# Spreading the inverse roots of the token norms by two r32 matmuls over a split diagonal, at other places among the tiles

## The chip, the cores and the metric

The kernel runs on one core of a Trainium2 chip. The metric is the device time of one execution in microseconds (us). Engines are named as in the profile: PE is TensorE (PEld its weight loads), DVE is VectorE, ACT is ScalarE, POOL is GpSimd, SP is SyncE, which issues the large DMAs.

## The reference, cut to what matters

512 tokens of width 1024 pass two transformer blocks in float32. What matters here is the shape that all of its norms have: a matrix product of the normalised activations, with the factor of each token pulled out of the product.

```python
def rms_norm(x, g):
    xf = x.astype(jnp.float32)
    y = xf * lax.rsqrt(jnp.mean(xf * xf, axis=-1, keepdims=True) + EPS)
    return (y * g.astype(jnp.float32)).astype(x.dtype)
...
        h = h + 0.5 * swiglu(rms_norm(h, ffn1_norm[i]), ffn1_w_gate[i], ffn1_w_up[i], ffn1_w_down[i])
        u = rms_norm(h, mix_norm[i])
        z = u @ w_in[i]
...
        gate = jax.nn.sigmoid(rms_norm(h, ple_norm[i]) @ w_ple_gate[i])
        h = h + gate * (p[i] @ w_ple_proj[i])
    return rms_norm(h, final_norm)
...
        x = x + mixers[layer % N_MIXERS](rms_norm_2(x, norm1[layer]))
        x = x + conv_ffn(rms_norm_2(x, norm2[layer]), *ffns[layer])
    return rms_norm_2(x, final_norm)
```

The mixer that is used in the second block is gated linear attention (GLA): it projects to q, k, v, a gate, and a 16-wide `a_low`, from which a second product makes the decay.

## The kernel before, in words

**Layout and precision.** Activations stand feature-major: 8 chunks (KD) of 128 features in the partitions, 512 tokens (S) in the free dimension. Each product of full precision is made of three r32 matmuls (`mm3`, L1644 to L1646): low weights by high input, high weights by low input, high by high. Weights come by DMA in slabs of 128x1024 into a ring of four (`w_raw`). ACT rounds a slab to its high part (`hi_part`, L681), POOL subtracts it for the low part in two pieces of 128x512 (`lo_part`, L594, both inputs in SBUF), and PE waits for `lo_ready` of the slab that a tile uses. A tile is 128 output features by 512 tokens, 24 matmuls, in one of four PSUM banks (`acc`); DVE evicts it and multiplies by the factor of each token (`rstd`).

**Order of the stages.** Feed-forward 1 up (44 tiles, the first four written out in `first_tiles`, L1759 to L1765), down, the mixing block in an order that is written by hand (`MIX`), feed-forward 2 up and down, the gates and the projection of the side input (`PLE_STEPS`: pgate 0, pgate 1, then eight short pproj tiles, then pgate 2 to 7), the GLA block in a hand-written order (`GLA`: gva, gk 0, alpha, gq 0, ...), feed-forward 3. Each engine walks through the same lists with semaphores between them.

**The norm of a token.** The squares are summed over the chunks by ACT and DVE; `sums(k)` on PE adds up the partitions token by token (L1655), in four columns of PSUM, so that the root is a short operation: ACT takes the square root, DVE makes the inverse root of 128x4 with a Newton step (`newton`, L1061 to L1065) in `tok_out`, a slice of PSUM. To bring it back into the form `rstd[any partition, token]`, DVE multiplies the identity by it (`spread_diag`, L1074: inputs `ident` in SBUF and `tok_out` in PSUM, output 128x512), and one fp32 matmul of ones by this diagonal matrix spreads it over all partitions (`spread(k)`, L1666). DVE copies it from PSUM to `rstd` (L1084). This is done for the norms k = 0 (before feed-forward 1), 1 (mixing), 3 (PLE gate) and 4 (GLA, which has two factors and so two diagonals and two matmuls). The other norms (`sums` with L1657, and the last one) are not touched by the change.

**Where the spreads stand.** PE goes on with tiles whose eviction needs the factor, and puts the spread among them:

- k = 0 in `first_tiles`, in tile 3 behind the low-input matmul of chunk 6 (`SPREAD_AT`).
- k = 1 in the mixing block, tile kk, ahead of chunk 6 (`mix_tile`, L1862 on).
- k = 3 in pgate 1 ahead of chunk 6 (`between` of `fm_tile`).
- k = 4 in tile gk 0 ahead of chunk 6, behind the transposes of `alow_k` (`turn_alow`, L2006). DVE makes its two diagonals between the evictions of token groups 1 and 2 of gva (evictions at L1509 and L1510).

Behind gk 0 comes `alpha`: four fp32 matmuls of 16 rows (L2036) that need `alow_ready`, a DVE copy of the transposed `alow` (L1512) that follows the gva evictions on DVE. DVE then copies `rstd` (L1514) and evicts gk 0 (L1537) and alpha (L1518).

**The start.** POOL sets `ones` and two columns of `eps` (L586 to L588, each one count of `consts_set`); PE waits for three counts and runs 16 warming matmuls on `ones` (L1840) ahead of the first tile.

Of the kernel before, what the change touches and what calls it, by code (L numbers as in the profile page):

```python
# [16 lines left out]
F32 = mybir.dt.float32  # L17
# [6 lines left out]
P = 128  # L24
# [24 lines left out]
SUMS_AT = (2, 5)  # L49
SPREAD_AT = (3, 6)  # L50
BANKS = 4
# [137 lines left out]
def layer_program(nc, A, out):  # L189
# [12 lines left out]
    with ExitStack() as ctx:  # L202
# [16 lines left out]
        rstd = sb("rstd", [P, S])  # L219
        ones = sb("ones", [P, P], side="right")  # L220
        cols = sb("cols", [P, NCOLS], side="right")
        consts = sb("consts", [P, NCONST], side="right")
        eps = sb("eps", [P, 2], side="right")
        rstd_tok = sb("rstd_tok", [P, NT], side="right")
        small = sb("small", [P, 176], side="right")
        gate_t, up_t, sq = tmp[:, 0:2, :], tmp[:, 2:4, :], tmp[:, 4:6, :]
        gres, ssum2 = side[:, 0, :], side[:, 1, :]
# [236 lines left out]
        def square(k, e):  # L464
            return tmp[:, e % 6, :] if k == 0 else sq[:, e % 2, :]

        def piece(p):

            return slice(2 * p * P, (2 * p + 2) * P)
# [115 lines left out]
        def _(pool):  # L585
            pool.memset(ones[:, :], 1.0).then_inc(consts_set, 1)  # L586
            pool.memset(eps[:, 0:1], NORM_EPS).then_inc(consts_set, 1)
            pool.memset(eps[:, 1:2], GN_EPS).then_inc(consts_set, 1)  # L588

            def lo_part(slot, width, count):  # L590
# [428 lines left out]
        def _(dve):  # L1019
# [52 lines left out]

            def spread_diag(i, tok):
                return dve.tensor_tensor(sq[:, i, :].rearrange("p (a b) -> p a b", a=NT), ident.unsqueeze(1).to_broadcast([P, NT, P]),  # L1074
                                         tok.unsqueeze(2).to_broadcast([P, NT, P]), ALU.mult)

            def rstd_by_token(roots, count, k):

                dve.wait_ge(root_ready, roots)
                link(inverse_root(tok_out[:, 0:NT], aux[:, 0, 0:NT], 1.0 / D, NORM_EPS, tok_ms[:, 0:NT], tok_root[:, 0:NT]))  # L1080
                spread_diag(0, tok_out[:, 0:NT]).then_inc(diag_ready, 1)
                dve.tensor_copy(rstd_tok[:, :], tok_out[:, 0:NT])
                dve.wait_ge(rstd_spread, SPREAD.index(k) + 1)
                dve.tensor_copy(rstd[:, :], aux[:, 1, :]).then_inc(rstd_ready, 1)  # L1084
                dve.wait_ge(rstd_ready, count)
# [410 lines left out]
            for step in GLA:  # L1496
# [5 lines left out]
                if kind == "gva":  # L1502
                    for tt in range(NT):
                        bank = acc[:, (t + tt) % BANKS, :]
                        if tt == 2:
                            spread_diag(0, tok_out[:, 0:NT])
                            spread_diag(1, tok_out[:, NT:2 * NT]).then_inc(diag_ready, 1)
                        dve.wait_ge(tile_done, t + tt + 1)
                        dve.tensor_scalar(alow_k[:, tt, :], bank[:, G_DV:GVA], rstd_tok[:, tt:tt + 1], None, ALU.mult)  # L1509
                        dve.tensor_scalar(gvt[:, 0, tt, :], bank[:, 0:G_DV], rstd_tok[:, tt:tt + 1], None, ALU.mult).then_inc(tile_freed, 1)  # L1510
                    dve.wait_ge(alow_turned, 1)
                    dve.tensor_copy(alow_t[0:G_RANK, :], aux[0:G_RANK, 3, :]).then_inc(alow_ready, 1)  # L1512
# [112 lines left out]
        def _(pe):  # L1625
# [36 lines left out]
            def spread(k):  # L1662

                pe.wait_ge(diag_ready, SPREAD.index(k) + 1)
                for i in range(2 if k == 4 else 1):
                    last = pe.matmul(aux[:, 1 + i, :], ones[:, :], sq[:, i, :], start=True, stop=True)  # L1666
                last.then_inc(rstd_spread, 1)
# [169 lines left out]
            HIDDEN = [KF, 2 * KF, 3 * KF + 2]  # L1837
            pe.wait_ge(consts_set, 3)
            for _ in range(WARM):
# [6 lines left out]
            def mix_tile(step, upto):  # L1846
# [28 lines left out]
                for c in range(first, upto):  # L1875
                    if step == ("kk",) and c == 6:
                        spread(1)
                    if step == ("wout", 0):
                        pe.wait_ge(split_ready, nth(lo_steps, (("mg", c), 0)) + 1)
                    last = mm3(o, (n % RING, blk(c)), x_hi[:, c, :], x_lo[:, c, :], c == 0, c == KD - 1)  # L1880
# [109 lines left out]
            for step in PLE_STEPS:  # L1990
                n, t = plan.first[step]
                if step[0] == "pgate":
                    fm_tile(t, [(n, b) for b in range(KD)], u_hi, u_lo, (lambda c: (u_ready, KD * 3 + c + 1)) if step[1] == 0 else None,
                            (lambda: spread(3)) if step[1] == 1 else None, u_used if step[1] == KD - 1 else None)
                    if step[1] == 0:
                        sums(3)
                else:
                    pe.wait_ge(hid_ready, 2 * KF + 2)
                    for i in range(4):
                        fm_tile(t + i, [(n, 2 * i), (n, 2 * i + 1)], p_hi, p_lo)  # L2000

            def turn_alow():
# [5 lines left out]
                free_when[3] = (alow_ready, 1)  # L2008
                spread(4)

            for step in GLA:
                kind = step[0]
                n, t = plan.first[step]
                if kind == "gva":
                    turns = [(k, tt) for k in range(2) for tt in range(NT - 1)] + [(k, NT - 1) for k in range(2)]
                    for k, tt in turns + [(k, tt) for k in range(2, KD) for tt in range(NT)]:
# [12 lines left out]
                        if k == KD - 1:  # L2029
                            last.then_inc(tile_done, 1)  # L2030
                elif kind == "alpha":
                    pe.wait_ge(alow_ready, 1)
                    pe.wait_ge(ple_loaded, 32)
# [186 lines left out]
```

## Time and profile before

| | |
|---|---|
| time, median of 3 runs | 1864.77 us (1863.76 to 1864.80) |
| time of the profiled execution | 1862.73 us |
| its span in the profile | 1860.9 us |
| PE busy | 1840.0 us, 99% |
| PE weight loads | 1498.0 us, 80% |
| DVE, ACT, POOL busy | 43%, 37%, 49% |
| mean granted clock of PE | 0.999 |
| chain that ended last | PE 96%, DVE 2%, ACT 1% |

The profiled execution is one run; 1.8 us of its time lie around the span. The start column of a timeline is in us from the start of the span, and the duration of a matmul is longer than the distance to the next start, because matmuls overlap: what a matmul costs PE is read from start to start. A merged row ("x6") has the time from the start of its first to the end of its last instruction. A released wait stands in brackets with the engine that ended it.

### The profile page before, as it was taken

How to read it: one execution, taken by the hardware profiler on the slowest of the kernel's cores; microseconds unless marked ns; L12 is line 12 of the kernel's file. 1: busy time of each engine (PE TensorE's matmuls, PEld its weight loads, DVE VectorE, ACT ScalarE, POOL GpSimd, SP SyncE). 2: the span in 40 equal slices, each digit the busy share in tenths (PEclk: the TensorE clock that was granted, in tenths of full speed). 3: DMA queues.
4: the chain of work that ended last, by engine and by line, in shares of the span. 5: the costliest groups of instructions: out<-in, count | busy, mean ns of one | idle time of the engine just before them, and what ended most of it. 6: DMA issues, size and time to landing. Idle time of an engine off the chain costs nothing.

```text
span 1860.9 us, 23896 instructions
## 1 busy us (share of the span) xinstructions
PE 1840.0 (99%) x8624; PEld 1498.0 (80%) x8624; DVE 793.1 (43%) x1297; ACT 679.4 (37%) x930; POOL 909.5 (49%) x710
## 2 busy tenths in 40 slices
PE   9999999999999999999999999999999999999998
PEld 8888888886878658888888888888877888888887
DVE  6222236215666653244222212266756374545312
ACT  5322223222232652244434422246344344444222
POOL 5544445386667424454444445353423455454542
PEclk9999999999999999999999999999999999999999
DMA  5333233243322212232232233232222222323331
GB/s 186 102 101 101 87 100 103 72 131 103 106 85 86 85 46 90 92 102 91 98 98 97 87 97 101 87 107 77 80 68 69 91 96 96 101 90 99 94 95 53
DMA packets 55093, 174.58 MB, mean 94 GB/s; under 512 B 6369, under 2 KB 10721, under 8 KB 55025
## 3 DMA queue, kind: packets, MB, share of 16 engines
q1 hardware_dynamic: 54848, 173.37, 29.4%
q8 instruction: 44, 0.72, 0.2%
q10 hardware_dynamic: 176, 0.30, 0.1%
q14 instruction: 25, 0.20, 0.0%
HBM read 166.56 MB, written 2.10 MB: 91 GB/s over the span
## 4 chain that ended last, share of the span: by engine, by line
PE 96%; DVE 2%; ACT 1%; issue 0%; DMA 0%; DVEq 0%; POOL 0%; ACTq 0%; POOLq 0%
PE acc L1644 28%; PE acc L1645 28%; PE acc L1646 28%; PE acc L1749 1%; PE acc L1751 1%; PE acc L1750 1%; PE aux L1927 1%; PE aux L1957 1%; PE acc L2079 0%; PE acc L2074 0%; PE acc L1978 0%; PE aux L1916 0%; PE aux L2065 0%; PE acc L1765 0%; PE acc L1759 0%
## 5 line engine op out<-in xcount | busy, mean ns | idle before, releaser
L594 POOL TENSOR_TENSOR w_lo<-w_raw,w_hi 128x512 fp32r<-128x512 f32 x626 | 812.6, 1321 | 911.4 <-ACT w_hi L681 911.4
L1644 PE MATMUL acc<-u_hi,w_lo 128*128 128x512 f32 x1544 | 611.7, 396 | 0.0
L1645 PE MATMUL acc<-u_lo,w_hi 128*128 128x512 f32 x1544 | 601.8, 390 | 0.0
L1646 PE MATMUL acc<-u_hi,w_hi 128*128 128x512 f32 x1544 | 601.8, 390 | 0.0
L681 ACT ACTIVATE w_hi<-w_raw 128x1024 fp32r<-128x1024 f32 (+2 forms) x313 | 321.8, 1033 | 549.6 <-PE acc L1646 472.1
L1644 PEld LDWEIGHTS acc<-u_hi,w_lo 128*128 128x128 f32 x1544 | 290.2, 188 | 71.9 <-issue 10.0
L1645 PEld LDWEIGHTS acc<-u_lo,w_hi 128*128 128x128 f32 x1544 | 290.3, 188 | 61.3 <-issue 2.6
L1646 PEld LDWEIGHTS acc<-u_hi,w_hi 128*128 128x128 f32 x1544 | 290.2, 188 | 61.2
L1644 PE MATMUL acc<-hid_hi,w_lo 128*128 128x512 f32 (+1 forms) x550 | 209.6, 381 | 0.0
L1645 PE MATMUL acc<-hid_lo,w_hi 128*128 128x512 f32 (+1 forms) x550 | 209.3, 380 | 0.0
L1646 PE MATMUL acc<-hid_hi,w_hi 128*128 128x512 f32 (+1 forms) x550 | 209.3, 380 | 0.0
L1644 PEld LDWEIGHTS acc<-hid_hi,w_lo 128*128 128x128 f32 x550 | 103.4, 188 | 19.8
L1645 PEld LDWEIGHTS acc<-hid_lo,w_hi 128*128 128x128 f32 x550 | 103.4, 188 | 19.8
L1646 PEld LDWEIGHTS acc<-hid_hi,w_hi 128*128 128x128 f32 x550 | 103.4, 188 | 19.7
L1102 DVE TENSOR_TENSOR tmp<-acc,rstd 128x512 f32<-128x512 f32 x43 | 29.7, 691 | 190.2 <-PE acc L1646 190.2
L1223 DVE SCALAR_TENSOR_TENSOR h<-acc,h 128x512 f32<-128x512 f32 x23 | 15.9, 691 | 220.5 <-PE acc L1646 220.5
L726 ACT ACTIVATE hid_hi<-tmp 128x512 f32 (+1 forms) x44 | 27.8, 633 | 211.8 <-DVE tmp L1093 211.8
L756 ACT ACTIVATE tmp<-tmp,cols 128x512 f32<-128x512 f32 x44 | 35.9, 816 | 116.2 <-DVE tmp L1130 116.2
L1130 DVE TENSOR_TENSOR tmp<-acc,rstd 128x512 f32<-128x512 f32 x44 | 30.3, 691 | 94.8 <-PE acc L1646 94.8
L1100 DVE TENSOR_TENSOR tmp<-acc,rstd 128x512 f32<-128x512 f32 x43 | 29.7, 691 | 90.5 <-PE acc L1646 90.3
L1044 DVE SCALAR_TENSOR_TENSOR u_lo<-h,cols,u_hi 128x512 fp32r<-128x512 f32 x40 | 42.6, 1076 | 36.5 <-ACT u_hi L699 29.3
L1749 PE MATMUL acc<-w_hi,u_lo 128*128 128x256 f32 x192 | 55.1, 287 | 0.0
(332 smaller groups left out, 2110.5 us busy)
## 6 DMA issues: line engine op xcount, KB each, us to landing
w_raw<-in_w_up SPq DMA_DIRECT2D x132, 512.0 KB, 3.4
w_raw<-in_w_mix SPq DMA_DIRECT2D x67, 512.0 KB, 3.8
w_raw<-in_w_down SPq DMA_DIRECT2D x48, 512.0 KB, 3.5
w_raw<-in_w_gla SPq DMA_DIRECT2D x30, 512.0 KB, 3.3
w_raw<-in_w_down SPq DMA_DIRECT2D x24, 384.0 KB, 3.1
w_raw<-in_w_ple SPq DMA_DIRECT2D x10, 512.0 KB, 3.8
tmp<-tmp SPq DMA_DIRECT2D x36, 64.0 KB, 2.0
h<-in_xT SPq DMA_DIRECT2D x8, 256.0 KB, 6.1
```

The lines of the kernel that those rows point to most:

```text
L594: ins = pool.tensor_tensor(w_lo[:, slot, part], w_raw[:, slot, part], w_hi[:, slot, part].bitcast(F32), ALU.subtract)
L681: act.activation(w_hi[:, slot, 0:width], w_raw[:, slot, 0:width], ACT.Copy).then_inc(hi_ready, 1)
L726: act.activation(hid_hi[:, i2 + b, :], up_t[:, b, :], ACT.Copy).then_inc(prod_hi, 1)
L756: act.activation(dst, (z_gate, z_up)[part][:, 2:2 + S], ACT.Identity, scale=conv_col("conv_w2", i2, p, part), bias=conv_col("conv_b", i2, ...
L1044: dve.scalar_tensor_tensor(u_lo[:, c, :], h[:, c, :], gain, u_hi[:, c, :].bitcast(F32), ALU.mult, ALU.subtract).then_inc(u_ready, 1)
L1100: dve.tensor_tensor(gate_t[:, b, :], acc[:, (t0 + 2 * b) % BANKS, :], rstd[:, :], ALU.mult).then_inc(tile_freed, 1)
L1102: dve.tensor_tensor(up_t[:, b, :], acc[:, (t0 + 2 * b + 1) % BANKS, :], rstd[:, :], ALU.mult).then_inc(tile_freed, 1)
L1130: dve.tensor_tensor((z_gate, z_up)[part][:, 2:2 + S], acc[:, (t0 + c) % BANKS, :], rstd[:, :], ALU.mult).then_inc(tile_freed, 1)
L1644: pe.matmul(o, w_lo[:, slot, columns], x_hi, start=first, stop=False)
L1645: pe.matmul(o, w_hi[:, slot, columns], x_lo, start=False, stop=False)
L1646: return pe.matmul(o, w_hi[:, slot, columns], x_hi, start=False, stop=last)
L1749: pe.matmul(o, u_lo[:, k, blk(tt)], w_hi[:, slot, columns], start=k == 0, stop=False)
```

## The change

The diagonal is made twice, from the high and the low part of the factors, and spread by two r32 matmuls that accumulate in the same bank. The factors of a token are split by two short DVE operations (`split_tok`) into `tok_part`, which lies in SBUF. The diagonals lie in large tensors that are not in use at that time. A copy of `ones` in r32 is made by POOL at the start. The spreads stand later among the tiles, and the diagonals of k = 4 behind all four gva evictions.

```diff
-SPREAD_AT = (3, 6)
+SPREAD_AT = (3, 7)
...
+        ones_r = sb("ones_r", [P, P], F32R, side="right")
+        tok_part = sb("tok_part", [P, 4 * NT], F32R, side="right")
...
+        def diag_part(k, i, part):
+
+            return (hid_hi, yr_hi, None, gy_hi, gy_hi)[k][:, 2 * i + part, :]
...
             pool.memset(eps[:, 1:2], GN_EPS).then_inc(consts_set, 1)
+            pool.wait_ge(consts_set, 1)
+            pool.tensor_copy(ones_r[:, :], ones[:, :]).then_inc(consts_set, 1)
...
-            def spread_diag(i, tok):
-                return dve.tensor_tensor(sq[:, i, :].rearrange("p (a b) -> p a b", a=NT), ident.unsqueeze(1).to_broadcast([P, NT, P]),
+            def split_tok(i, tok):
+
+                hi, lo = (tok_part[:, (2 * i + j) * NT:(2 * i + j + 1) * NT] for j in range(2))
+                link(dve.tensor_copy(hi, tok))
+                return dve.tensor_tensor(lo, tok, hi.bitcast(F32), ALU.subtract)
+
+            def spread_diag(k, i, part):
+                tok = tok_part[:, (2 * i + part) * NT:(2 * i + part + 1) * NT].bitcast(F32)
+                return dve.tensor_tensor(diag_part(k, i, part).rearrange("p (a b) -> p a b", a=NT), ident.unsqueeze(1).to_broadcast([P, NT, P]),
                                          tok.unsqueeze(2).to_broadcast([P, NT, P]), ALU.mult)
...
-                spread_diag(0, tok_out[:, 0:NT]).then_inc(diag_ready, 1)
+                link(split_tok(0, tok_out[:, 0:NT]))
+                spread_diag(k, 0, 0)
+                spread_diag(k, 0, 1).then_inc(diag_ready, 1)
...
                     for tt in range(NT):
                         bank = acc[:, (t + tt) % BANKS, :]
-                        if tt == 2:
-                            spread_diag(0, tok_out[:, 0:NT])
-                            spread_diag(1, tok_out[:, NT:2 * NT]).then_inc(diag_ready, 1)
...
+                    split_tok(0, tok_out[:, 0:NT])
+                    link(split_tok(1, tok_out[:, NT:2 * NT]))
+                    spread_diag(4, 0, 0)
+                    spread_diag(4, 0, 1)
+                    spread_diag(4, 1, 0)
+                    spread_diag(4, 1, 1).then_inc(diag_ready, 1)
                     dve.wait_ge(alow_turned, 1)
...
                 for i in range(2 if k == 4 else 1):
-                    last = pe.matmul(aux[:, 1 + i, :], ones[:, :], sq[:, i, :], start=True, stop=True)
+                    for part in range(2):
+                        last = pe.matmul(aux[:, 1 + i, :], ones_r[:, :], diag_part(k, i, part), start=part == 0, stop=part == 1)
                 last.then_inc(rstd_spread, 1)
...
-            pe.wait_ge(consts_set, 3)
+            pe.wait_ge(consts_set, 4)
...
-                    if step == ("kk",) and c == 6:
+                    if step == ("iq", 0) and c == 1:
                         spread(1)
...
                     fm_tile(t, [(n, b) for b in range(KD)], u_hi, u_lo, (lambda c: (u_ready, KD * 3 + c + 1)) if step[1] == 0 else None,
-                            (lambda: spread(3)) if step[1] == 1 else None, u_used if step[1] == KD - 1 else None)
+                            None, u_used if step[1] == KD - 1 else None)
...
                 else:
+                    if step[1] == 0:
+                        spread(3)
                     pe.wait_ge(hid_ready, 2 * KF + 2)
...
                 free_when[3] = (alow_ready, 1)
-                spread(4)
...
                 elif kind == "alpha":
+                    spread(4)
                     pe.wait_ge(alow_ready, 1)
```

## Rows read from the trace of the kernel before

**Rows 1.** The page: busy time by engine, and the chain that ended last.

```profile
PE 1840.0 (99%) x8624; PEld 1498.0 (80%) x8624; DVE 793.1 (43%) x1297; ACT 679.4 (37%) x930; POOL 909.5 (49%) x710
PE 96%; DVE 2%; ACT 1%; issue 0%; DMA 0%; DVEq 0%; POOL 0%; ACTq 0%; POOLq 0%
```

**Rows 2.** Spread and diagonal by line: duration min/median/max in ns, first and last start.

```profile
L1666 PE MATMUL aux<-tmp,ones x10: 590/592/697, 29.1 to 1283.2; 128*128 128x512 f32 x10
L1074 DVE TENSOR_TENSOR tmp<-consts,aux x5: 678/686/686, 27.1 to 1278.2; 128x512 f32<-128x512 f32 x5
```

**Rows 3.** Timeline of PE, k = 0: start, duration, line, tile, count.

```profile
29.11 1.02 PE L1666 MATMUL aux<-tmp,ones 128*128 128x512 f32 x2
...
30.20 0.40 PE L1762 MATMUL acc<-u_lo,w_hi 128*128 128x512 f32 x1
30.43 0.62 PE L1765 MATMUL acc<-u_hi,w_lo 128*128 128x512 f32 x2
31.01 0.49 PE L1644 MATMUL acc<-u_hi,w_lo 128*128 128x512 f32 x1
```

**Rows 4.** Timeline of DVE and POOL around the spread of k = 0.

```profile
26.94 0.17 DVE L1065 TENSOR_TENSOR aux<-aux,small 128x4 f32<-128x4 f32 x1
27.14 0.69 DVE L1074 TENSOR_TENSOR tmp<-consts,aux 128x512 f32<-128x512 f32 x1
...
28.34 5.47 POOL L594 TENSOR_TENSOR w_lo<-w_raw,w_hi 128x512 fp32r<-128x512 f32 x4 [9.79 <-ACT w_hi L681]
...
30.90 3.47 DVE L1108 TENSOR_TENSOR tmp<-tmp,rstd 128x512 f32<-128x512 f32 x2
```

**Rows 5.** Timeline of the start, and of the sums of k = 0.

```profile
0.75 0.20 POOL L586 MEMSET ones<- 128x128 f32 x1 [0.29 <-POOLq L2210]
...
1.07 6.28 PE L1840 MATMUL aux<-ones 128*128 128x128 f32 x32 [1.07 <-POOL eps L588]
...
24.44 0.97 PEld L1655 LDWEIGHTS aux<-ones,ssum 128*128 128x128 f32 x8 [0.27 <-DVE ssum L1052]
```

**Rows 6.** Timeline around the spread of k = 1.

```profile
371.63 10.00 POOL L594 TENSOR_TENSOR w_lo<-w_raw,w_hi 128x512 fp32r<-128x512 f32 x8 [13.77 <-ACT w_hi L681]
...
377.07 0.17 DVE L1065 TENSOR_TENSOR aux<-aux,small 128x4 f32<-128x4 f32 x1
...
378.91 1.02 PE L1666 MATMUL aux<-tmp,ones 128*128 128x512 f32 x2
```

**Rows 7.** Timeline around the spread of k = 3.

```profile
1211.58 7.53 POOL L594 TENSOR_TENSOR w_lo<-w_raw,w_hi 128x512 fp32r<-128x512 f32 x6 [0.88 <-ACT w_hi L681]
...
1215.30 0.69 DVE L1074 TENSOR_TENSOR tmp<-consts,aux 128x512 f32<-128x512 f32 x1
...
1215.20 0.39 PE L1646 MATMUL acc<-u_hi,w_hi 128*128 128x512 f32 x1
1216.04 1.12 PE L1666 MATMUL aux<-tmp,ones 128*128 128x512 f32 x2 [0.45 <-DVE tmp L1074]
...
1218.38 0.40 PE L1644 MATMUL acc<-p_hi,w_lo 128*128 128x512 f32 x1
```

**Rows 8.** Timeline around the spread of k = 4 and alpha.

```profile
1277.63 1.28 DVE L1074 TENSOR_TENSOR tmp<-consts,aux 128x512 f32<-128x512 f32 x2
...
1279.50 0.48 DVE L1510 TENSOR_SCALAR gvt<-acc,rstd_tok 128x256 f32<-128x256 f32 x1
...
1278.74 7.47 POOL L594 TENSOR_TENSOR w_lo<-w_raw,w_hi 128x512 fp32r<-128x512 f32 x6 [7.95 <-ACT w_hi L681]
...
1281.91 1.88 PE L1666 MATMUL aux<-tmp,ones 128*128 128x512 f32 x4
...
1285.12 3.70 PE L2036 MATMUL acc<-alow_t,walpha 16*128 16x512 f32 x8
```

**Rows 9.** A DVE operation with two inputs in SBUF, three in a row, by line.

```profile
L1182 DVE SCALAR_TENSOR_TENSOR tmp<-rstd,tmp x12: 691/1662/1670, 269.7 to 317.3; 128x512 f32<-128x512 f32 x12
```

**Rows 10.** Windows: busy time by engine; the third number from the end is the granted clock.

```profile
1289.00:1293.00 4.00, 4.00 (x12) 3.09 (x12) 2.23 (x5) 3.75 (x6) 0.00 (x0) 0.58 0.41 131
```

## The prediction

> **What bounds the kernel now.** I read the page first: PE is busy 99% of the span, and the chain that ended last runs 96% on PE [rows 1]. So work taken off PE is worth its full time, and work added elsewhere counts only where PE comes to wait for it. The total is no help for a change of five instructions, so I went on to the lines of the spread and of the diagonal: ten records of the fp32 spread (two for each of five matmuls) and five diagonals at 0.69 us [rows 2]. Then I read the timeline at each of the four places, on PE for what the spread costs, on DVE and POOL for when the diagonal is ready [rows 3 to 8].
>
> **The matmul itself.** At k = 0 the spread starts at 29.11; the second matmul behind it starts at 30.20 [rows 3]. Of these 1.09 us the plain matmul between them takes 0.23, the step from 30.20 to 30.43, so the fp32 spread costs 0.86, two r32 matmuls of the same columns 0.46, and each spread saves 0.40 us. Five give 2.0 us. This is an upper bound for what the arithmetic can bring, 0.11% of the time.
>
> **What DVE now has in front of a spread.** Before: one diagonal behind the last step of the root. After: a copy and a subtraction of 128x4, each ending in a wait on DVE itself, about 0.20 each by the step from one such operation to the next (26.94 to 27.14 [rows 4]), then two diagonals. There is a second difference. The factor used to be read from PSUM (`tok_out`), now from `tok_part` in SBUF, so the diagonal has two inputs in SBUF. At k = 3 the old diagonal took 0.69 while POOL was in the middle of six low-part pieces [rows 7]. The operations with two SBUF inputs behave otherwise: three in a row take 0.69 and then 1.66 and 1.67 us [rows 9], and the two at 30.90, with POOL running, take 3.47 together [rows 4]. I take 0.69 us for a diagonal with POOL idle and 1.67 with POOL busy. The bounds of four are 2.8 and 6.9 us.
>
> The Trainium skill, page "SBUF — State Buffer", section on the ports, says that a DVE operation with two SBUF inputs and a GpSimd operation that reads SBUF take one port pair in turn, each for its whole length, and that the other blocks fully. The rows agree in kind. With a whole low-part piece of about 1.26 us (7.53 for six [rows 7]) in every gap it would make 1.95 us of a diagonal, not 1.67; by that the sum below would be about 1.5 us higher.
>
> **k = 0.** POOL copies `ones` to r32 ahead of PE's start. The fill of the same tile took 0.20, the copy is not in the trace; a quarter of a two-input piece of 128x512 would be about 0.34, and a semaphore hop comes on top: 0.3 to 0.5, which shifts the warming matmuls and the first tiles. PE waited 0.27 at the sums for DVE [rows 5], which takes this up but for 0.1 us (0 to 0.25). The factor is done at 27.11, so the diagonals run from 27.55 to about 28.84. PE reaches the new place two matmuls later, 29.3: no wait. But POOL wants to start the pieces of slab 4 at 28.34 and meets the second diagonal, which costs it 0.5. PE would be through tile 3 at 30.89 before (two matmuls from 30.43) and started tile 4 at 31.01: it waited for just these pieces (28.34 plus two of about 1.3, [rows 4]). So the 0.40 saved on PE brings nothing here, and the 0.5 is PE's. Sum +0.6 (from -0.1 if POOL is not held up, to +0.75).
>
> **k = 1.** The factor is done at 377.24, the diagonals begin at 377.7 amid eight pieces of POOL that last until 381.63 [rows 6], so two take 1.4 to 3.3: ready between 379.1 and 381.0. The new place is behind c = 6 and 7 of kk and c = 0 of iq 0, nine matmuls or 2.04 us behind 378.91: 380.95. No wait, or a tenth. `rstd` comes some 1.6 us later, but a bank is wanted again only three tiles of 24 matmuls (5.5 us) behind. -0.4 (to -0.2).
>
> **k = 3.** PE had finished c = 5 at 1215.43 and waited until 1216.04. Now it does the six matmuls of c = 6 and 7 and is at the spread at 1216.8. The diagonals begin at 1215.7, POOL works until 1219.1 [rows 7]: ready at 1217.1 at best, 1219.1 with 1.67 each. I take 1218.9, with one wait for a piece already under way. The spread and the restart cost 0.6, so pproj starts at about 1219.5 in place of 1218.38: **+1.1** (-0.7 to +1.4). A wait of 0.6 is replaced by one of 2.1.
>
> **k = 4.** Before, the two diagonals stand between the evictions and take 1.28 [rows 8]. Without them the last eviction ends 1.28 earlier, at 1278.7. Both splits take 0.8: 1279.5. Then four diagonals, with POOL's six pieces from 1278.74 to 1286.2, longer if they meet: 1282.2 at best, 1286.2 at worst; I take 1285.8, since the stream of pieces covers all four. PE ends gk 0 at 1283.3 (six matmuls from 1281.91) and stands ahead of alpha with the spread: it waits 2.5 us. Then 0.92 for four r32 matmuls and a restart of 0.1: alpha begins at 1286.85, before 1285.12: **+1.7** (-0.9 to +2.1). The copy of `alow` is behind the diagonals on DVE and ends at 1286.5, just in time; `rstd` and the eviction of gk 0 follow 2 to 3 us later than before, and the fourth alpha matmul, which wants that bank, comes some 2.7 us behind the first: no further wait. POOL's pieces come up to 2 us later; they are for tiles behind alpha.
>
> **Sum:** 0.6 - 0.4 + 1.1 + 1.7 = +3.0 us. The profiled execution took 1862.73 us with a span of 1860.9, so it would take 1865.7. It is 2.04 under the median of the three runs; on the median it is 1867.8.
>
> **Rival A, slower: the clock.** Behind alpha, whose 16-row matmuls take PE 3.7 us, the granted clock is 0.58 over four us [rows 10]: 3.4 us at 1.2 GHz, which is half of 2.4, so 1.7 us lost. After the change the thin stretch is 2.5 us of waiting, then the spread, then alpha. If a second such stretch follows, or one at the 2.1 us wait of k = 3, the same price comes again: +4.7 in all, 1869.5; with both, 1871.2. For it: the thin stretch is twice as long as the one that did it. Against: the spread in its middle is dense work, and one fall may cover the whole. [...]
>
> **Rival B, no collision.** If the diagonals run at 0.69 (a broadcast of four columns may not hold the port as a full tile does, or POOL's pieces lie elsewhere), the terms are 0.0, -0.4, -0.7 and -0.9: -2.0 us, 1862.8. For it: rows 9 and 4 are of full tiles, none of a broadcast one. Against: POOL is in mid-stream at three of four places.
>
> **Rival C, faster.** As B, and alpha reached without a wait at another point of the clock's rhythm, so that the stretch of rows 10 does not come: -3.7, 1861.1.
>
> A measurement of this kernel can tell about 0.2%, 3.7 us, from no change. That the change does not do what it says is no case here: the spread must be r32 to be split.
>
> **How the numbers follow.** Forecast (+3.0) 0.36; A 0.30; B 0.23; C 0.06; the rest, mainly waits that I have not seen, 0.05. Slower by over 0.2% needs +3.7: most of A and a fifth of the forecast, 0.33. Faster: most of C, 0.05. Same: 0.62. The range takes in B and most of A: 1862.3 to 1870.8; the forecast's own is 1866.3 to 1869.3.
>
> **What would show it.** The spread as ten r32 records, each 0.23 behind the last. New diagonals (ten, not five) with a median near 1.67; at 0.69 B holds. PE's wait for the diagonal of about 2 us at pproj and 2.5 ahead of alpha; none at k = 0 and 1. Tile 4 starting at about 31.6. The granted clock below 1 behind alpha for 3.4 us in the forecast, for twice that in A. I am wrong if the waits at k = 3 and 4 are under 1 us, or if PE waits later, for an eviction that needs `rstd`.

## The result, and the profile after

The changed kernel takes 1871.76 us in the median of six runs (1869.14 to 1872.35); the kernel before, run beside it, took 1864.26 (1862.90 to 1866.50). The ratio is 1.0037, with a 95% interval of 1.0027 to 1.0047: slower, by 7.5 us between the two medians. The prediction was 1867.8, range 1862.3 to 1870.8. The direction and the wait terms were about right, the size was 4 us too small, and the time lies 1 us above the range. The profiled execution took 1872.35 us with a span of 1870.5, against 1860.9 before.

The page after, busy time by engine and the chain that ended last (to be read against [rows 1]):

```profile
PE 1843.3 (99%) x8624; PEld 1499.4 (80%) x8624; DVE 803.8 (43%) x1312; ACT 679.4 (36%) x930; POOL 914.0 (49%) x711
PE 91%; DVE 3%; POOL 2%; ACT 2%; issue 1%; DMA 1%; SPq 0%; DVEq 0%; ACTq 0%; POOLq 0%
```

PE is busy for longer than before although less arithmetic is asked of it, and the chain now leaves PE for DVE and POOL. DVE has 15 more instructions (five diagonals and ten operations of the splits) and is busy for 10.7 us longer.

The diagonals and the r32 spreads by line: count, duration min/median/max in ns, first and last start ([rows 2] before).

```profile
L1089 DVE TENSOR_TENSOR gy_hi<-consts,tok_part x6: 1483/1748/1777, 1217.7 to 1288.5; 128x512 fp32r<-128x512 f32 x6
L1089 DVE TENSOR_TENSOR hid_hi<-consts,tok_part x2: 682/687/692, 28.7 to 29.3; 128x512 fp32r<-128x512 f32 x2
L1089 DVE TENSOR_TENSOR yr_hi<-consts,tok_part x2: 1303/1538/1773, 378.6 to 379.8; 128x512 fp32r<-128x512 f32 x2
L1687 PE MATMUL aux<-gy_hi,ones_r x6: 395/400/499, 1220.9 to 1291.1; 128*128 128x512 f32 x6
```

The r32 matmuls are as cheap as foreseen. Only the two diagonals of k = 0 still take 0.69 us; both began before POOL's first piece, which then paid (1.64 us for that piece). At k = 3 and 4 they take 1.48 to 1.78.

The timeline of the changed kernel at its four places, and at the value projection of 422 us that no step of the prediction looked at (start, duration, engine, line; [rows 3, 4], [rows 6], [rows 7], [rows 8] before):

```profile
28.67 1.29 DVE L1089 TENSOR_TENSOR hid_hi<-consts,tok_part 128x512 fp32r<-128x512 f32 x2
29.47 6.28 POOL L602 TENSOR_TENSOR w_lo<-w_raw,w_hi 128x512 fp32r<-128x512 f32 x4 [9.78 <-ACT w_hi L689]
30.66 0.62 PE L1687 MATMUL aux<-hid_hi,ones_r 128*128 128x512 f32 x2
32.49 0.50 PE L1664 MATMUL acc<-u_hi,w_lo 128*128 128x512 f32 x1 [0.74 <-POOL w_lo L602]
...
378.62 3.00 DVE L1089 TENSOR_TENSOR yr_hi<-consts,tok_part 128x512 fp32r<-128x512 f32 x2
382.40 0.62 PE L1687 MATMUL aux<-yr_hi,ones_r 128*128 128x512 f32 x2
383.05 0.69 DVE L1101 COPY rstd<-aux 128x512 f32<-128x512 f32 x1 [1.36 <-PE aux L1687]
387.06 2.54 POOL L602 TENSOR_TENSOR w_lo<-w_raw,w_hi 128x512 fp32r<-128x512 f32 x2 [3.04 <-ACT w_hi L689]
421.71 0.69 DVE L1317 TENSOR_TENSOR tmp<-acc,rstd 128x512 f32<-128x512 f32 x1 [3.16 <-POOL q L636]
422.46 0.42 PE L1883 MATMUL acc<-w_hi,u_lo 128*128 128x328 f32 x1 [1.11 <-DVE tmp L1317]
...
1217.68 3.15 DVE L1089 TENSOR_TENSOR gy_hi<-consts,tok_part 128x512 fp32r<-128x512 f32 x2
1213.57 8.40 POOL L602 TENSOR_TENSOR w_lo<-w_raw,w_hi 128x512 fp32r<-128x512 f32 x6 [0.92 <-ACT w_hi L689]
1220.88 0.73 PE L1687 MATMUL aux<-gy_hi,ones_r 128*128 128x512 f32 x2 [1.98 <-DVE gy_hi L1089]
1221.45 0.39 PE L1664 MATMUL acc<-p_hi,w_lo 128*128 128x512 f32 x1
...
1283.64 6.60 DVE L1089 TENSOR_TENSOR gy_hi<-consts,tok_part 128x512 fp32r<-128x512 f32 x4
1283.31 11.74 POOL L602 TENSOR_TENSOR w_lo<-w_raw,w_hi 128x512 fp32r<-128x512 f32 x8 [9.45 <-ACT w_hi L689]
1290.29 1.21 PE L1687 MATMUL aux<-gy_hi,ones_r 128*128 128x512 f32 x4 [2.27 <-DVE gy_hi L1089]
1291.42 7.19 PE L2059 MATMUL acc<-alow_t,walpha 16*128 16x512 f32 x8
```

At k = 3 and k = 4 PE stands in front of the spread for 1.98 and 2.27 us, for diagonals that run beside POOL's low parts; POOL is slowed too (six pieces in 8.40 us, in [rows 7] 7.53). And alpha's matmuls take 7.19 us in place of 3.70 [rows 8]. Windows show why (as in [rows 10], the third number from the end is the granted clock, 0.50 being 1.2 GHz and 1.00 being 2.4):

```profile
1275.00:1277.00 2.00, 1.86 (x17) 1.67 (x16) 0.41 (x1) 0.00 (x0) 0.00 (x0) 1.00 0.64 242
1278.00:1281.00 3.00, 3.00 (x15) 3.00 (x15) 1.25 (x9) 0.18 (x1) 0.00 (x0) 0.50 0.00 0
1284.00:1290.00 6.00, 4.02 (x20) 2.91 (x18) 6.00 (x4) 2.19 (x3) 6.00 (x5) 1.00 0.25 89
1292.00:1301.00 9.00, 9.00 (x14) 3.97 (x13) 5.09 (x10) 3.43 (x5) 3.04 (x3) 0.50 0.41 134
```

The clock is at 1.2 GHz from 1277.7 to 1281.1, behind the one-column sums of k = 4, and from 1291.3 to 1301.6. I call 3.4 us at 1.2 GHz one fall, as that is the length of the one in [rows 10]: this is one fall and then three in a row.

**Where the 7.3 us are.** One profile is not enough to tell falls from the rest, so the kernel before was profiled four times and the changed one three times (the repeats are among the experiments). I took the time between landmarks of PE in each and compared the means. From PE's first warming matmul to its last sum the changed kernel is 7.0 us longer, and its warming begins 0.3 later. The pieces, in us:

| stretch of PE | after less before | forecast |
|---|---|---|
| start, to the sums of k = 0 | +0.5 | +0.1 |
| k = 0, sums to tile 4 | +0.34 | +0.5 |
| k = 1, sums to the value projection | -0.37 | -0.4 |
| value projection and what follows, to the logits | +0.84 | 0 |
| k = 3, sums to pproj | +1.09 | +1.1 |
| k = 4, sums to gk 0 (clock) | +1.50 | 0 |
| k = 4, alow to alpha | +0.96 (1.73, 0.57 and 0.56 against 0.00) | +1.7 |
| alpha to the next tiles (clock) | +3.42 | 0 |
| elsewhere (falls near 622 and 700 us; a wait near 1316 us, 0.35 in three of the four profiles before and gone after) | -1.0 | 0 |

The foreseen steps make +2.5 of a forecast +3.0. What was forecast at nothing makes the rest: the clock, +4.9 at two places, and the value projection, +0.84, less the 1.0 elsewhere.

### The profile page after: what moved, and what is told of

Same layout as the page of the kernel before. It is cut to its first block, busy times and chain, and to the rows that moved or that the text cites. A ratio compares the mean times of both kernels' runs of the same rounds, so it can differ in the third digit from the quotient of the medians.

```text
span 1870.5 us, 23912 instructions
## 1 busy us (share of the span) xinstructions
PE 1843.3 (99%) x8624; PEld 1499.4 (80%) x8624; DVE 803.8 (43%) x1312; ACT 679.4 (36%) x930; POOL 914.0 (49%) x711
## 4 chain that ended last, share of the span: by engine, by line
PE 91%; DVE 3%; POOL 2%; ACT 2%; issue 1%; DMA 1%; SPq 0%; DVEq 0%; ACTq 0%; POOLq 0%
PE acc L1664 27%; PE acc L1665 27%; PE acc L1666 27%; PE acc L1770 1%; PE acc L1771 1%; PE acc L1772 1%; PE aux L1948 1%; POOL w_lo L602 1%; PE aux L1978 1%; DVE gy_hi L1089 1%; PE acc L2102 0%; PE acc L2097 0%; PE acc L1999 0%; PE aux L1937 0%; PE aux L2088 0%
```

## The experiments

**Factors in PSUM.** The changed kernel, but the factor and its low part are read from PSUM, where only the low part needed a new place:

```
-                hi, lo = (tok_part[:, (2 * i + j) * NT:(2 * i + j + 1) * NT] for j in range(2))
+                hi, lo = tok_part[:, 2 * i * NT:(2 * i + 1) * NT], tok_lo[:, i * NT:(i + 1) * NT]
...
-                tok = tok_part[:, (2 * i + part) * NT:(2 * i + part + 1) * NT].bitcast(F32)
+                tok = (tok_lo if part else tok_out)[:, i * NT:(i + 1) * NT]
```

> The changed kernel, with the factors that the diagonals read left in PSUM: the high diagonal reads the unsplit factor and is rounded as it is written, the low one reads a low part that the subtraction writes to PSUM. Everything else stands where the change put it. Collision theory (a diagonal with both inputs in SBUF takes turns with POOL's low parts, which costs PE its waits at k = 3 and k = 4): all ten diagonals near 0.69 us, PE's wait ahead of pproj from 2.0 to under 0.4, ahead of alpha from 2.3 to none; POOL starts its pieces of slab 4 unhindered. PE's own terms are worth about 0.35 + 1.8 + 2.6 us, so some 4.7 us less than the changed kernel, near 1867. Rival (the clock): the falls of the granted clock cost 5 us more than before and are set off by the waits; then the clock of the stretch from alpha on also recovers and the time is near 1864 or under. Rival (the late place of the spreads does it): the time stays within 1.5 us of 1871.8.

It took 1863.8 us (11 runs), as the kernel before: ratio 1.0001, interval 0.9992 to 1.0010. That is 3 us under what the collision alone was expected to give, and what the rival with the clock gave: in its profile no fall stands at alpha (one is at the sums of k = 4). Its diagonals by line, and its waits for the two causes in question (engine, tile and line, what it waited for: total, times, longest):

```profile
L1089 DVE TENSOR_TENSOR gy_hi<-consts,aux x6: 680/681/686, 1218.1 to 1284.2; 128x512 fp32r<-128x512 f32 x6
L1089 DVE TENSOR_TENSOR yr_hi<-consts,aux x2: 680/683/686, 377.5 to 378.1; 128x512 fp32r<-128x512 f32 x2
```

```profile
PE aux L1861 <- POOL ones_r L596: 1.4, 1, 1.4
PE acc L1883 <- DVE tmp L1317: 1.0, 1, 1.0
```

With the one input moved from SBUF to PSUM, all ten diagonals are at 0.68 us in the same mid-stream of POOL, and no wait for a diagonal is left. In its profile k = 3 is 0.87 and k = 4 0.80 us shorter than before. So the collision is a matter of where the four columns lie. The wait at the value projection stays: it does not come from slow diagonals. The warming matmuls' wait for the copy of the ones stays as well, and the first sums still come at 25.05 us, no later than in three of the four profiles of the kernel before (25.04 to 25.10): that copy costs nothing that can be told from the scatter of the start.

**The SBUF factor alone.** The kernel before, fp32 spreads at the old places, one diagonal each, but the factors copied to SBUF ahead of it:

```
+                tok = tok_sb[:, i * NT:(i + 1) * NT]
...
+                link(dve.tensor_copy(tok_sb[:, 0:NT], tok_out[:, 0:NT]))
```

> The kernel before with one thing of the change alone: the factors are copied to SBUF and the five fp32 diagonals read them there. One fp32 matmul at the old places, no split. Collision theory: diagonals at k = 1, 3 and 4 between 1.3 and 1.8 us in place of 0.69, that of k = 0 (POOL idle then) stays 0.69; PE's wait at k = 3 grows from 0.5 to about 1.6 us, at k = 1 a wait of 0.2 appears, none at k = 4, where the diagonals have two microseconds of slack: +1.3 us in all. Rival (a broadcast of four columns does not hold the port, the slow diagonals come from the r32 output): all five stay at 0.69 and the time is that of before.

1865.48 us (11 runs), ratio 1.0011, interval 1.0002 to 1.0020. The diagonals by line, and the wait:

```profile
L1076 DVE TENSOR_TENSOR tmp<-consts,tok_sb x5: 684/693/1657, 28.1 to 1282.1; 128x512 f32<-128x512 f32 x5
```

```profile
PE aux L1670 <- DVE tmp L1076: 1.6, 1, 1.6
```

But for a short copy in front, nothing but the operand's place differs here. The diagonals of k = 1 and 3 take 1.55 and 1.66 us. Those of k = 4, which the expectation had slow too, take 0.69: POOL begins its next pieces only at 1282.44, when they are almost done. k = 3 is 1.13 us longer. So an SBUF factor costs k = 3 as much without r32, a second diagonal or a new place as with all three (1.09).

**r32 at the old places.** As the first, with the spreads of k = 0, 1 and 4 where they stood before (that of k = 3 stays ahead of pproj, where the change put it), k = 4's diagonals between the evictions, and PE waiting for the r32 ones only behind its warming:

```
-                    if step == ("iq", 0) and c == 1:
+                    if step == ("kk",) and c == 6:
...
+                spread(4)
...
-                    spread(4)
```

> r32 spreads over split diagonals with the factors in PSUM, and the spreads of k = 0, 1 and 4 at their places of before (k = 4 with its four diagonals between the evictions of gva); k = 3 stays ahead of pproj; PE waits for the r32 ones only behind its warming matmuls. Theory: k = 0 brings nothing (PE waits for slab 4), k = 1 0.4 us, k = 3 0.7, k = 4 0.8, no wait at rva: 1.9 us under before, which is at the edge of what can be told. Rival (late rstd and clock): if the time lies over before, the r32 spread has a cost of its own that I have not named. The granted clock should be as before, one fall behind alpha.

1863.7 us (11 runs), ratio 0.9996, interval 0.9987 to 1.0005. The 1.9 us under the kernel before that were expected did not come; the part on the prediction says why. In two profiles of it PE waits 0.1 us at most at the value projection, and from there to the logits it takes 0.15 us less than before, against 0.84 more in the changed kernel. So that wait belongs to the later place of the spread of k = 1. No version that I ran has a lower median, and it does not beat the kernel before by anything that the runs can tell.

**Filler ahead of alpha.** The changed kernel with ten dense r32 matmuls of 512 columns, whose sums nobody reads, in the time in which PE waited ahead of the spread of k = 4:

```
+                    for i in range(10):
+                        pe.matmul(o, ones_r[:, :], u_hi[:, i % KD, :], start=True, stop=True)
```

> The changed kernel with ten r32 matmuls of 512 columns (2.3 us, results thrown away: each starts a new sum in a bank of alpha, which alpha overwrites) in front of the spread of k = 4, in the time in which PE waits for the diagonals. Clock theory (the wait of 2.3 us in front of alpha sets off or prolongs the fall of the granted clock): alpha's eight matmuls take 3.7 us again and not 7.2, and the time falls by about 3.3 us to 1868.5. Rival (alpha's matmuls of 16 rows set it off by themselves, as before the change): the fall begins where it began or a little later, alpha is slow as before or slow in part, and the time changes by less than 1 us.

1868.93 us (6 runs), ratio 1.0031, interval 1.0019 to 1.0043. The timeline of PE:

```profile
1287.49 2.50 PE L2056 MATMUL acc<-u_hi,ones_r 128*128 128x512 f32 x10
1289.83 1.09 PE L1687 MATMUL aux<-gy_hi,ones_r 128*128 128x512 f32 x4
1290.86 3.69 PE L2062 MATMUL acc<-alow_t,walpha 16*128 16x512 f32 x8
```

Filled, the wait costs PE the same time as in the changed kernel's first profile (and 1 us more than in its two others, below); alpha begins only 0.56 us earlier, and alpha runs at full clock; one fall comes behind it (1295.2 to 1298.6) in place of three. Against the kernel before it is 5.1 us slower, the changed one 7.5, but the two intervals overlap: whether the filler gains any time is not shown by these runs. The next one says more.

**PSUM at k = 4 only.** The changed kernel with the factors of the last pair alone read from PSUM (their low part is written there too):

```
...
+                if k == 4:
+                    tok = (tok_lo if part else tok_out)[:, i * NT:(i + 1) * NT]
```

> The changed kernel with one difference: only the fourth stage's factors (high and low, of the pair y and gy at the spread before alpha) are read from PSUM; the factors of k = 0, 1 and 3 stay in SBUF. Theory (the four diagonals at k = 4, slowed to 1.65 us each, hold TensorE for 2.3 us in front of alpha's 16-row matmuls, and the idle time together with them brings the run of clock falls): the wait of PE at the spread of k = 4 goes, alpha comes 1.7 to 2.6 us earlier, at most one fall is left at alpha, and the time is 1866 to 1867.5 us, about 2 over the kernel before: what is left is k = 3's wait of 2.0 us (+1.1) and the 0.7 at k = 0. The wait of 1.0 at the value projection on tmp stays (k = 1 is unchanged). Rival (the falls are a matter of chance from execution to execution and the wait in front of alpha has no part in them): only the 1.7 to 2.6 us of the wait go and the falls stay: 1869 to 1870. Rival (all of the loss sits at k = 3 and before): no change, 1871.

1867.71 us (11 runs), ratio 1.0015, interval 1.0006 to 1.0024, which lies wholly below the changed kernel's: 3.1 us over the kernel before in place of 7.5. That is 0.2 above the time that the theory allowed, and below what its rivals gave. Its timeline of PE at k = 4:

```profile
1288.97 1.10 PE L1691 MATMUL aux<-gy_hi,ones_r 128*128 128x512 f32 x4
1290.00 4.39 PE L2063 MATMUL acc<-alow_t,walpha 16*128 16x512 f32 x8
```

The wait in front of alpha is gone, as expected, but two falls stand at alpha (1292.9 to 1299.7), where I had expected one at most, and another at 1221.2, behind the wait of k = 3. So the wait ahead of alpha is not what brings falls there, or not alone. The 3.1 us that still divide this kernel from the one with all factors in PSUM (which is level with the kernel before) are mostly k = 0 and k = 3, the falls apart: in the two profiles 0.34 and 2.05 us of PE's steps.

**The changed kernel twice more.**

> The changed kernel unaltered, a second profile of it. If the three falls of the clock behind alpha belong to the program (a wait of 2.3 us and then 16-row matmuls), they stand at the same place again, with the one behind the one-column sums at k = 4, and the span is 1869.5 to 1871. If they are a matter of chance, one or two of them are missing and the span is 1866 to 1868. The start: sums of k = 0 at 1.1 us later than in the profile before if that belongs to the copy of ones, 0.6 to 1.0 if it is only the landing of x.

> The changed kernel, a third profile. The falls behind alpha were three with a wait of 2.3 us in front of it and two with a wait of 1.1; the four diagonals took 6.60 and 5.78 us. If the diagonals' time goes with where GpSimd's low parts happen to stand, it lies again between 5.6 and 6.7 us and the wait goes with it; two or three falls at alpha. The wait of 1.1 us at the value projection and the one of 2.0 at k = 3 are there again, as they hang on the program and not on chance.

1869.39 and 1870.12 us. The diagonals and the wait of k = 4 in the second profile:

```profile
1283.17 5.78 DVE L1089 TENSOR_TENSOR gy_hi<-consts,tok_part 128x512 fp32r<-128x512 f32 x4
1289.01 1.20 PE L1687 MATMUL aux<-gy_hi,ones_r 128*128 128x512 f32 x4 [1.11 <-DVE gy_hi L1089]
1290.13 5.35 PE L2059 MATMUL acc<-alow_t,walpha 16*128 16x512 f32 x8
...
1283.18 1.85 POOL L602 TENSOR_TENSOR w_lo<-w_raw,w_hi 128x512 fp32r<-128x512 f32 x1 [9.46 <-ACT w_hi L689]
```

The third is the same (5.78, wait 1.10). So a collision has no fixed price: with the same program the four took 6.60 once and 5.78 twice, and the wait halves. The difference is the first of the four: in the first profile POOL began its piece 0.33 us ahead of it and it took 1.52; in the two others it began level with POOL or 0.01 ahead and took 0.69, and POOL's piece took 1.85 in the second. The waits of k = 3 (2.0) and of the value projection (1.1) came back unchanged in both. At alpha there are two falls in each, and one at the sums of k = 4; so the third fall of the first profile is not there in every execution.

**The kernel before three times more.**

> The kernel before unaltered, a second profile of it. It gives the scatter of the places that the ledger is made against: the start of the first sums (27.3 us in the first profile), and the falls of the clock (one behind alpha at 1289 to 1293 in the first). If the landing of x was early in the first profile, the first sums start 0.5 to 1.0 us later here. If the falls wander, the one at alpha is gone or another stands at the transposes near 700 us or behind the sums at 1277 us.

> The kernel before, a third profile. Two profiles of it have no fall of the clock behind the one-column sums of k = 4 (1277 to 1281 us), eight of eight of the other kernels have one, which costs 1.5 us. If that is chance, a third and a fourth profile of before should show one; if something in every changed kernel brings it, both show none and the first norm projection of k = 4 starts 4.9 us behind those sums as in the first two.

> The kernel before, a fourth profile, with the same expectation as the third: a fall behind the sums of k = 4 if it is chance, none and 4.9 us from those sums to the first norm projection if the changed kernels bring it.

1862.95, 1863.64 and 1864.01 us. None of the three has a fall at the sums of k = 4 or at alpha; each has one near 622 or 700 us, where PE had waited 1.7 or 1.5 us in attention. The first sums stand 0.6 us later than in [rows 5] in all three, so the first profile began early (its first sums are at 24.44 us in [rows 5]; the 27.3 of the expectation is a slip). Windows of the third, at the sums and behind alpha:

```profile
1274.00:1278.00 4.00, 3.85 (x32) 3.66 (x32) 1.47 (x8) 0.18 (x1) 0.00 (x0) 1.00 0.34 117
1288.00:1296.00 8.00, 8.00 (x31) 5.34 (x29) 4.63 (x8) 6.55 (x11) 2.66 (x3) 1.00 0.46 152
```

**r32 at the old places, again.**

> The kernel of e3_r32_old_places, a second profile. If its missing wait in front of alpha is what keeps the clock up there, no fall or one at alpha again; with two, as in e5_psum_k4_only, which has no such wait either, the falls at alpha are told by chance more than by the wait.

1863.52 us, no fall at alpha, one at the sums of k = 4. Its windows:

```profile
1273.00:1275.00 2.00, 1.85 (x17) 1.77 (x16) 0.16 (x1) 0.00 (x0) 0.00 (x0) 1.00 0.63 225
1276.00:1278.00 2.00, 2.00 (x11) 2.00 (x10) 1.06 (x6) 0.06 (x1) 0.00 (x0) 0.50 0.00 0
1292.00:1301.00 9.00, 9.00 (x60) 8.26 (x59) 4.34 (x7) 8.92 (x13) 0.53 (x1) 1.00 0.19 60
```

**Alpha broken up.** As r32 at the old places, with the last two alpha tiles among the matmuls of gq 0, so that the 16-row work is not in a row:

```
+                    for c in range(KD):
+                        if c in (2, 4):
+                            alpha_tile(1 + c // 2)
```

> The kernel of e3_r32_old_places with alpha's four 16-row matmuls no longer in a row: two stand first, the other two among the matmuls of gq 0. Theory (thin work of TensorE lets the clock fall, each fall costs 1.5 to 1.7 us): no fall at alpha, as in e3, and nothing else moves: the one at the sums of k = 4 is still there, 1863.0 to 1864.0, no difference from e3 that can be measured. If alpha's matmuls had a share in falls in e3's other executions, the median goes down to 1862 to 1863. Rival (the later alpha rows hold up what reads them): 1864.5 or more.

1869.45 us (7 runs), ratio 1.0028, interval 1.0017 to 1.0039. The rival came true, dearer than it said: PE waits for what DVE makes from the decay. The wait, of this kernel:

```profile
PE aux L2102 <- DVE gsc L1585: 5.0, 1, 5.0
```

It ends at 1319.3 us, behind DVE's scans, and the clock is at 1.2 GHz from 1318.5 to 1325.3, two falls. Alpha is the head of a chain through DVE and ACT, and to hold back half of it is dear. No fall stands at alpha itself, but none did in the kernel that it was made from; on thin work it tells nothing.

## Why the prediction was wrong where it was

**The matmul itself: right.** The two of a pair start 0.23 us apart and each spread saves 0.4: the -0.37 of k = 1 comes through whole.

**Two SBUF inputs beside POOL: right, and now shown.** The prediction took 1.67 us for a diagonal in POOL's stream; k = 3 and 4 have 1.48 to 1.78. The operand's place alone makes it (PSUM 0.68 for all ten, SBUF alone up to 1.66 in the kernel before). Rival B, that a broadcast of four columns would not hold the port, is refuted. The Trainium skill, page "SBUF — State Buffer", section on the ports, has the conflict, for an operation of two tensors on DVE, only when both inputs are in SBUF, which is what the move to PSUM bears out; the 1.95 us that the prediction worked out for a whole piece in every gap was not measured.

**k = 0: +0.34 for +0.5, right in its mechanism.** POOL's piece met the second diagonal, and tile 4 waited 0.74 us for it. The +0.1 for the copy of the ones can't be told from the start's own scatter.

**k = 1: the step that failed first.** The prediction said that rstd is late but "a bank is wanted again only three tiles of 24 matmuls (5.5 us) behind" (5.5 us is one such tile). True of the banks of the tiles in hand, and beside the point: rstd also feeds a chain on other engines. Set against the sums of k = 1, the copy of rstd stands 1.6 us later (383.05 against 379.97, less the 1.44 by which all is later there). The copies of the cosines and sines make up some of it. The eviction of srg stands 0.94 later (384.67 against 382.29, less 1.44), then ACT's silu and its high part w_hi behind that, then POOL's low parts. The kernel before, at POOL's low parts and at the last rotated eviction:

```profile
384.67 2.53 POOL L594 TENSOR_TENSOR w_lo<-w_raw,w_hi 128x512 fp32r<-128x512 f32 x2 [3.04 <-ACT w_hi L681]
...
419.35 0.69 DVE L1300 TENSOR_TENSOR tmp<-acc,rstd 128x512 f32<-128x512 f32 x1 [3.18 <-POOL q L628]
```

After, these stand at 387.06 and 421.71, both 2.4 us later, while PE arrives only 1.07 later: POOL's rotations and low parts, one behind the other over 35 us with one wait of 2.8 us for a DMA that is as late, carry the lateness undiminished to the eviction for which PE then waits 1.11, or 1.27 from start to start. A later wait on ACT shrinks by 0.37 for it; with some hundredths from smaller ones +0.84 is left. The prediction looked for who wants the bank, not for who else stands behind the late operation.

**k = 3: right.** +1.09 for +1.1, with a wait of 1.98 for 2.1.

**k = 4: right in kind, over-sized on average.** Alpha was later by 1.73 in the first profile and by 0.57 and 0.56 in the others, for +1.7. The term assumed every diagonal in collision for its whole length; that is what happened once in three.

**The clock: the term that made the difference, and a rival mis-sized.** The sum gave it nothing. Rival A gave it one more fall of 1.7 us, or two, with a chance of 0.30. What came is a fall at the sums of k = 4, where nobody had looked (+1.50), and at alpha 3, 2 and 2 falls against 1, 0, 0 and 0 before (+3.42). Two errors are in it. The ledger was made against a single profile that happened to hold one fall at alpha; and "one fall may cover the whole" was an unfounded ceiling on a stretch of thin work that, slowed, becomes twice as long. A wait of 1.1 us in front of alpha had two falls, and a kernel with no wait there had two as well. That the 1871.2 of rival A lies near the measured time is luck: its second fall was to come at the wait of k = 3, where none of the three profiles of the changed kernel has one.

**Where the falls come.** The 14 profiles show a regularity. In each, every change of the clock stands a whole number of fall lengths behind its first rise to 2.4 GHz (which comes at 4.3 to 6.8 us); I call these moments marks. In the profile of the kernel with PSUM at k = 4 only, three stretches at 1.2 GHz begin 17 and 4 fall lengths apart:

```profile
1221.19:1224.60 3.41, 3.41 (x10) 2.65 (x9) 2.61 (x4) 2.02 (x3) 0.61 (x2) 0.50 0.43 155
1279.21:1282.63 3.42, 3.42 (x17) 3.42 (x16) 2.07 (x10) 0.18 (x1) 0.00 (x0) 0.50 0.00 0
1292.87:1299.69 6.82, 6.82 (x15) 4.22 (x14) 3.13 (x6) 5.69 (x9) 1.52 (x2) 0.50 0.47 154
```

The same thin work stands at another distance behind the last mark in another profile, and the falls go with this distance, without an exception in the 14 (us behind the last mark, number of profiles):

| thin work of PE | with a fall | without |
|---|---|---|
| sums of k = 4 (1.9 us) | 0.38 to 1.49 (10) | 2.31 to 3.31 (4, all of the kernel before) |
| wait of 1.74 near 622 us | 1.42 to 1.47 (3) | to 0.65, and from 2.10 (11) |
| wait of 1.49 near 700 us | 1.32 to 1.61 (5) | to 1.16, and from 1.97 (9) |
| alpha, no wait for the spread ahead of it | 0.54, 2.02, 2.31, 2.48 (4) | 1.18 to 1.91 (6) |
| alpha, behind a wait of 1.1 | 1.45, 1.51 (2) | none |

(Left out at alpha are the first profile of the changed kernel, whose fall begins with alpha, behind a wait of 2.27, and alpha broken up.) By these rows the fall at the sums goes with their place between the marks, and what PE gains or loses ahead of them moves that place: +1.50 is then no price of an r32 spread in itself, and the kernel with fp32 spreads and an SBUF factor has that fall too. At alpha the wait counts as well: at 1.43 without a wait there is no fall, at 1.45 and 1.51 behind a wait of 1.1 there are two.

**What stays open.** This was read from the profiles afterwards. No run moved the work between the marks on purpose, and four profiles can't tell how often the kernel before has its sums at a place with a fall (nine of 46 runs of it were at a mean clock of 0.997, and may have had one). What is shown is the price: whoever has the fall at the sums takes about 1.5 us longer there. It also explains why r32 spreads without a collision win nothing: in the PSUM kernel at the old places, k = 1, 3 and 4 save 0.37, 0.81 and 0.79, the transposes of k = 4 come some 0.27 later behind the four diagonals, and the fall gives 1.53 back.

## What to carry over

An operand that moves from PSUM to SBUF is a change of its own, however small it is: four columns turned 0.68 us into 1.5 to 1.8 beside a busy GpSimd, and undoing that alone removed the whole loss (in part because the falls at alpha went with it). When an operation gets later, follow everything that it stands in front of on its own engine and through the others, not just the buffer that it frees; a serial engine carries lateness over tens of microseconds. And with differences of some 0.2%, profile the kernel before several times first: the falls of the clock differ from one execution to the next, each is as large as a whole term, and a change that only shifts thin work by a microsecond can bring or remove one.

## What the runs showed of the hardware

- The granted clock had only the two levels, and every fall lasted 3.4 us or two or three times that. Over the 46 runs of the kernel before beside the experiments, the median time is 1863.15 us where the mean clock is 0.999 (17 runs), 1864.05 at 0.998 (20) and 1866.67 at 0.997 (9): most of the scatter of this kernel is the clock.
- The falls that I placed stand behind thin work on PE: one-column sums, 16-row matmuls, waits of 1.5 us and more. The Trainium skill, page "TensorE: Matmul & The Clock Gate", section "What's actually happening", says that the gate looks at activity in windows that run freely and don't begin with the kernel. The table of places bears that out: the same thin work has a fall or not by where it stands between the changes of the clock, at 622 and 700 us as at the sums of k = 4.
- GpSimd pays in a collision as well: six low parts in 8.40 us at k = 3 for 7.53 before. At k = 4 the first diagonal took 0.69 us where it began ahead of POOL's piece or level with it, and 1.52 where it began 0.33 us behind.
